# The order of gates, context turns, projection passes and scores in a fused two-block kernel

## The reference, cut to what matters

```python
def first_block(x, mem, ...):
    for i in range(DEPTH):                      # layer A, then layer B
        h = rmsnorm(x, norm_w[i])
        mix, q_mem, gate = gla_mixer(h, ...) if i % 2 == 0 else dilated_mixer(h, ...)
        mem_o = memory_attention(q_mem, mem_n, w_memkv[i])          # softmax(q_mem k) v
        branch = concatenate([mix, mem_o]) * silu(gate)
        x = x + branch @ w_out[i]
    return rmsnorm(x, final_norm_w)

def _layer(x, xc, ...):                          # second block, layer l = 0, 1
    h = _rms(x, g_pre) * (1.0 + scale) + shift                     # latent rows
    hc = _rms(xc, g_pre) * (1.0 + mod_c[1]) + mod_c[0]             # context rows
    ...                                          # h @ w_in, hc @ w_in, split by columns
    # differential attention: two score maps of 48 columns per head
    s1 = einsum('bqhd,bkhd->bhqk', a, k1) * scale
    s2 = einsum('bqhd,bkhd->bhqk', b, k2) * scale
    w = softmax(s1) - lam * softmax(s2)
    o = einsum('bhqk,bkhe->bqhe', w, v)          # then a norm per head, times silu(gate)
    y = concatenate([na, diff, conv]) @ w_out
    x_new = x + gate * _rms(y, g_post)           # and xc in the first layer
```

## Time and profile before

| | |
|---|---|
| median of 3 runs | 1652.66 us (1650.25 to 1654.98) |
| profiled execution | 1653.44 us |
| its span | 1651.6 us |
| mean granted clock of PE | 0.991 |
| PE busy | 1597.0 us (97%), 8870 matmuls |
| DVE busy | 979.8 us (59%) |
| ACT busy | 667.6 us (40%) |
| POOL busy | 140.7 us (9%) |
| mean DMA traffic | 98 GB/s |

### The profile page before, as it was taken

The page is one execution under the profiler, slowest core; times in us unless marked ns, Lnnn a source line. Parts: engine busy times, 40 slices in busy tenths (PEclk is TensorE's granted clock), DMA queues, the critical chain, the costliest instruction groups (busy, mean ns, idle before and its releaser), DMA issues.

```text
span 1651.6 us, 22948 instructions
## 1 busy us (share of the span) xinstructions
PE 1597.0 (97%) x8870; PEld 1277.7 (77%) x8870; DVE 979.8 (59%) x1803; ACT 667.6 (40%) x1323; POOL 140.7 (9%) x192
## 2 busy tenths in 40 slices
PE   7999999899999999999999999989999999999898
PEld 6977877687878878878888888865656887788676
DVE  1356454456556655665447787565665467876674
ACT  3365443424323323263313435244554325433653
POOL 4132100000000000002000110000112001000001
PEclk9999999899999999999999999999999999999899
DMA  8221244334654764462223111221003134213100
GB/s 289 81 77 50 103 153 117 80 82 121 190 158 120 155 185 139 148 151 68 92 96 109 56 54 40 92 93 58 1 26 96 48 107 140 58 39 128 52 14 39
DMA packets 171252, 161.36 MB, mean 98 GB/s; under 512 B 40374, under 2 KB 154280, under 8 KB 171112
## 3 DMA queue, kind: packets, MB, share of 16 engines
q1 hardware_dynamic: 151944, 126.97, 26.1%
q10 hardware_dynamic: 16928, 25.27, 4.7%
q0 software_dynamic: 2272, 7.64, 1.4%
HBM read 149.80 MB, written 11.18 MB: 97 GB/s over the span
## 4 chain that ended last, share of the span: by engine, by line
PE 83%; DVE 10%; ACT 4%; issue 2%; DMA 0%; POOL 0%; ACTq 0%; SPq 0%; POOLq 0%; DVEq 0%
PE psum L2596 46%; PE psum L2567 10%; PE psum L2630 7%; PE psum L3139 5%; PE psum L2621 4%; PE psum L3137 2%; PE psum L2775 2%; PE psum L2687 2%; PE psum L2730 2%; DVE arena L1999 1%; PE psum L2669 1%; PE psum L3010 1%; DVE arena L1969 1%; DVE wring_r L2076 1%; DVE arena L2133 1%
## 5 line engine op out<-in xcount | busy, mean ns | idle before, releaser
L2596 PE MATMUL psum<-hT_r,wring_r 128*128 128x512 f32 x1696 | 575.2, 393 | 3.6 <-ACT branch L1745 1.1
L2596 PEld LDWEIGHTS psum<-hT_r,wring_r 128*128 128x128 f32 x1696 | 319.3, 188 | 79.0 <-issue 10.0
L2596 PE MATMUL psum<-arena_r,wring_r 128*128 128x256 f32 (+1 forms) x1360 | 359.1, 333 | 0.7 <-ACT branch L1564 0.5
L1564 ACT ACTIVATE arena<-psum 128x512 f32<-128x512 f32 (+6 forms) x256 | 149.8, 611 | 416.0 <-PE psum L2596 244.2
L2596 PEld LDWEIGHTS psum<-arena_r,wring_r 128*128 128x128 f32 x1360 | 218.3, 190 | 26.2 <-issue 1.8
L2567 PE MATMUL psum<-arena 128*128 128x96 f32 (+9 forms) x1460 | 220.8, 365 | 16.9 <-ACT branch L1745 7.1
L2596 PE MATMUL psum<-arena_r 128*128 128x512 f32 (+1 forms) x720 | 224.5, 350 | 0.0
L2567 PEld LDWEIGHTS psum<-arena 128*128 128x128 f32 (+5 forms) x1460 | 160.8, 189 | 64.7 <-issue 31.9
L2596 PE MATMUL psum<-hT_r,arena_r 128*128 128x512 f32 x448 | 177.8, 397 | 1.8 <-DVE wring_r L2076 1.0
L2630 PE MATMUL psum<-ident,arena 128*128 128x128 f32 (+3 forms) x1104 | 145.9, 277 | 17.4 <-DMA arena<-in_c_ctx 7.4
L2630 PEld LDWEIGHTS psum<-ident,arena 128*128 128x128 f32 (+3 forms) x1104 | 125.2, 142 | 39.6 <-issue 14.6
(11 more groups left out here) (237 smaller groups left out, 1967.8 us busy)
## 6 DMA issues: line engine op xcount, KB each, us to landing
wring<-in_w_in_b SPq DMA_DIRECT2D x54, 512.0 KB, 5.9
arena<-in_w_mod ACTq DMA_DIRECT2D x16, 1536.0 KB, 8.3
wring<-in_w_in SPq DMA_DIRECT2D x16, 1536.0 KB, 6.9
wring<-in_w_out SPq DMA_DIRECT2D x8, 2048.0 KB, 8.4
wring<-in_w_in_a SPq DMA_DIRECT2D x5, 1536.0 KB, 6.6
arena<-x_dram SPq DMA_DIRECT2D x3, 2048.0 KB, 14.6
wring<-in_w_in SPq DMA_DIRECT2D x6, 1024.0 KB, 5.7
arena<-ebias_dram SPq DMA_DIRECT2D x144, 32.0 KB, 1.8
```

What stands on the lines that cost most here:

```text
L1564: return nc.scalar.activation(out, in_, ACT.Copy, scale=scale)
L2596: ins_ = nc.tensor.matmul(b[0:hi.shape[2], 0:width], w[:, k], v[:, k], start=k + p == 0, stop=(k, p) == (KT - 1, 2))
```

## The change

The diff has eight pieces, none of which changes what is computed:

1. Gate B 4 stands ahead of qm B in the step list, in place of behind it.
2. `final_rows(TT - 2)` on DVE is a step xr of its own ahead of hcT 0; it was part of xf behind it.
3. In layer 1 nv stands ahead of nq.
4. hcT 1 stands behind the last dT of layer 0's differential stage, in place of behind doT of the last row tile. The place from which weight slots are counted for layer 1 stays at that doT.
5. oN stands ahead of yv and the first part of yc, in place of behind them.
6. gate B 0 and the first output of nkc (at even k) run hi x hi and lo x hi as soon as the features' hi is there, and wait for their lo ahead of the third pass.
7. nk does the same for all k, in groups of three outputs.
8. dS claims and fills the banks of one map, then those of the other; before, both were claimed and then the two maps' matmuls alternated.

```diff
--- before.py
+++ after.py
@@ -198,10 +198,9 @@
     add("v" * 8, "wout", "A")
     modulation()
     add("v" * 8, "hT", "B")
-    for i in range(4):
+    for i in range(5):
         add("a", "gate", "B", i)
     add("av", "qm", "B")
-    add("a", "gate", "B", 4)
     add("a" * 8, "mS", "B")
     for g in range(2):
         add("aav", "Bproj", 0, g)
@@ -238,6 +237,7 @@
         add("va", "BPV", h)
     add("", "outs", "wout", "B", 0, (5,))
     add("v" * 6, "wout", "B")
+    add("", "xr")
     add("vvvv", "hcT", 0)
     add("", "xf")
     add("vv", "woutl", "B")
@@ -251,8 +251,11 @@
         for f in range(CF):
             add("av" + "av" * both, "cv", l, f)
         add("av" * 3, "nvF", l)
-        add(lat_ctx * 3, "nq", l)
+        if l == 0:
+            add(lat_ctx * 3, "nq", l)
         add("aaaavv", "nv", l)
+        if l:
+            add(lat_ctx * 3, "nq", l)
         neighbourhood(add, l)
         keys = [("av", "dF", l, "k", g) for g in range(3)]
         queries = [(lat_ctx, "dF", l, "q", g) for g in range(3)]
@@ -495,6 +498,8 @@
             if h == 0 and i:
                 projected(tiles[i - 1])
             add("a", "dT", l, t, h)
+            if n > len(items) and l == 0:
+                add("vvvv", "hcT", 1)
             if n == 4:
                 add("vv", "dv", l, 2)
             rows = [(tiles[i - 1], 1)] if h == 1 and i else [(t, 0)] if n == 5 or (h == DH - 1 and i) else []
@@ -508,6 +513,8 @@
         if n < len(items):
             add("aa", "dS", l, *items[n])
         beside(n)
+        if n >= 2 and h == 0 and i:
+            add("", "oN", l, tiles[i - 1])
         if n >= 2 and l:
             for half, q in YO_SPLITS.get(n, ()):
                 add("", "yv", half, q)
@@ -515,8 +522,6 @@
                 if part == 0:
                     add("", "yc", u, part)
         if n >= 2:
-            if h == 0 and i:
-                add("", "oN", l, tiles[i - 1])
             if h == 1 and i > 1:
                 add("", "yx", l, tiles[i - 2])
             if h == 2 and i > 1 and l == 0:
@@ -537,9 +542,7 @@
     if l == 0:
         add("", "nx", before)
     add("v", "doT", l, last)
-    if l == 0:
-        add("vvvv", "hcT", 1)
-    else:
+    if l:
         add("", "yx", l, before)
     add("v", "yo", l, last, 0, 1)
     add("v", "yo", l, last, 1, 1)
@@ -930,7 +933,7 @@
         split_list = [(key, g) for key, _ in steps for g in range(split_jobs(key))]
         split_at = {job: n for n, job in enumerate(split_list)}
         before_mem = split_at[("Bproj", 1, 0), 0]
-        split_starts = [("wout", "A"), ("wout", "B"), ("hcT", 1)]
+        split_starts = [("wout", "A"), ("wout", "B"), ("doT", 0, TT - 1)]
         split_bounds = [sum(split_jobs(key) for key, _ in steps[:order_of[start]]) for start in split_starts]
 
         def split_place(n):
@@ -2229,8 +2232,9 @@
                         free(nc.vector.scalar_tensor_tensor(branch[:, f], full(dve, key, f)[:, :],
                                                             vec[:, V_GLA + f % 3:V_GLA + f % 3 + 1], branch[:, f],
                                                             ALU.mult, ALU.mult))
+                elif kind == "xr":
+                    final_rows(TT - 2)
                 elif kind == "xf":
-                    final_rows(TT - 2)
                     norm_scale("C0", TT - 2)
                 elif kind in ("wout", "woutl"):
                     ph = key[1]
@@ -2588,11 +2592,17 @@
                 b = claim(pe, key, i) if 0 in blocks else bank(key, i)
                 new = {("gate", "B", 0): ("hT", "B")}.get(key)
                 for k in blocks:
+                    passes = ((hi, x_hi), (hi, x_lo), (lo, x_hi))
                     if key[0] == "nkc" and i == 0 and k % 2 == 0:
-                        evacuated(pe, ("hcT", key[1]), k // 2)
-                    if new and i == 0:
-                        evacuated(pe, new, k)
-                    for p, (w, v) in enumerate(((hi, x_hi), (hi, x_lo), (lo, x_hi))):
+                        turned, last_k, b_ = ("hcT", key[1]), k + 1, k // 2
+                    else:
+                        turned, last_k, b_ = new if i == 0 else None, k, k
+                    if turned:
+                        pe.wait_ge(hi_ready, hi_at(turned, last_k))
+                        passes = ((hi, x_hi), (lo, x_hi), (hi, x_lo))
+                    for p, (w, v) in enumerate(passes):
+                        if turned and p == 2:
+                            evacuated(pe, turned, b_)
                         ins_ = nc.tensor.matmul(b[0:hi.shape[2], 0:width], w[:, k], v[:, k], start=k + p == 0, stop=(k, p) == (KT - 1, 2))
                 if KT - 1 in blocks:
                     done(ins_)
@@ -2681,10 +2691,14 @@
                     parts = [split_weights(split_at[("nkc", l), g])[2:] for g in range(3)]
                     banks = [claim(pe, key, g) for g in range(3)]
                     for k in range(KT):
+                        pe.wait_ge(hi_ready, hi_at(("hT", f"C{l}"), k))
+                        for g, (hi, lo) in enumerate(parts):
+                            nc.tensor.matmul(banks[g], hi[:, k], hT_hi[:, k], start=k == 0, stop=False)
+                        for g, (hi, lo) in enumerate(parts):
+                            nc.tensor.matmul(banks[g], lo[:, k], hT_hi[:, k], start=False, stop=False)
                         evacuated(pe, ("hT", f"C{l}"), k)
                         for g, (hi, lo) in enumerate(parts):
-                            for p, (w, v) in enumerate(((hi, hT_hi), (hi, hT_lo2), (lo, hT_hi))):
-                                ins_ = nc.tensor.matmul(banks[g], w[:, k], v[:, k], start=k + p == 0, stop=(k, p) == (KT - 1, 2))
+                            ins_ = nc.tensor.matmul(banks[g], hi[:, k], hT_lo2[:, k], start=False, stop=k == KT - 1)
                             if k == KT - 1:
                                 done(ins_)
                         if k + HT_BANKS < KT:
@@ -3040,20 +3054,19 @@
                     evacuated(pe, ("dX", l, "q", t))
                     if (t, h) == (0, 0):
                         evacuated(pe, ("dX", l, "k", TT + CT - 1))
-                    for half in range(2):
-                        claim(pe, key, half)
                     tt = t % TT
                     rows = [slice(half * DPAD, half * DPAD + DD) for half in range(2)]
                     q = [dqT[t // TT][r, h, tt * P:(tt + 1) * P] for r in rows]
                     if t < TT:
-                        for part in range(2):
-                            cut = slice(part * KEYS // 2, (part + 1) * KEYS // 2)
-                            for half in range(2):
+                        for half in range(2):
+                            claim(pe, key, half)
+                            for part in range(2):
+                                cut = slice(part * KEYS // 2, (part + 1) * KEYS // 2)
                                 ins_ = product(psum[:, 2 * half + part, 0:KEYS // 2], [(q[half], dkT[rows[half], h, cut])])
-                                if part:
-                                    done(ins_)
+                            done(ins_)
                     else:
                         for half in range(2):
+                            claim(pe, key, half)
                             done(product(psum[:, 2 * half, 0:NMEM], [(q[half], dkT[rows[half], h, T:KEYS])]))
                 elif kind == "dT":
                     l, t, h = key[1:]
```

## The result

The changed kernel takes 1640.69 us (median, 1639.46 to 1641.01), the kernel before 1653.61 in the same comparison. The ratio is 0.992, with an interval of 0.9907 to 0.9934: 12.9 us faster. The forecast was 1640.2.

The account below looks back on a forecast made before the run. PE (TensorE, 83% of the chain) was taken as the bound. The terms -10.3 - 3.25 + 4.9 - 0.4 - 2.8 - 0.6 sum to -12.45 us, from a median of 1652.66 to 1640.2, range 1632 to 1650.

Parts of the forecast that it names:

- gate B 4 ahead of qm: Gate B to Bproj: weights load and are rounded earlier, Bproj starts at about 309.55 instead of 318.09; -10.3 us with the clock.
- rounded half first: gate B 0: Gate B 0: half of PE's 0.93 us wait for VectorE's low half goes; -0.45 us.
- nk, layer 0 and layer 1: First nk matmuls of each layer: six of nine run before the low half comes; -1.4 us per layer.
- final rows ahead of hcT 0: Block 1's final rows: one 1.3 us VectorE operation passes ahead of eight copy pairs; 0, up to 0.5 us cost.
- hcT 1 early: Border before layer 0's last output projection: PE stalls 3.4 us behind VectorE's pairs, lower clock costs 2.0; +4.9 us in all.
- nv ahead of nq: Layer 1 neighbourhood projections: 0.97 us wait for nv's low half replaced by about 0.6 for nvF's copy; -0.4 us.
- oN ahead of yv: Layer 1 differential stage: PE's 2.27 us wait for VectorE's normalisation goes, dT starts 2.4 earlier; -2.8 us.
- map by map: Differential scores: map 0 can run while PE waits for map 1's bank; -0.6 us in all.
- gain of 4 more: Differential scores: possible extra 4 us if the filled waits no longer bring the lower clock.
- (a): Rival: the border costs little and filled waits bring no lower clock; about 1633 us, chance 0.13.
- (b): Rival: Bproj's load is not earlier, as another semaphore than PE's read holds it; 1654.2 us, chance 0.06.
- (c): Rival: score maps lose their overlap, 1.1 us in each of 32 latent items; near 1675 us, chance 0.04.

Follow-up runs that it names:

- fourth experiment: Changed kernel with gate B 4 back behind qm B and the two roundings ahead of its silu moved behind the exponentials of mS: 1640.48 us.
- first two experiments: Changed kernel with hcT 1 back behind doT of the last row tile: 1635.08 us; changed kernel with hcT 1 one output half later: 1641.86 us.
- experiments 3 and 7: Kernel before with only gate B 4 ahead of qm B: 1641.76 us; changed kernel with oN behind yv and yc again: 1644.36 us.
- experiment 1: Changed kernel with hcT 1 back behind doT of the last row tile: 1635.08 us, timed again 1635.31 us.

## Why the prediction was right, point by point

The mechanism was right: PE is the bound, the chain from gate 4's last read to mS gave 10.7 of the 12.4 us of span, and the border took back what was foreseen. That the time was met within 0.5 us is in part luck. Several small terms came out wrong and cancelled (gate B 0, nkc, nv, the maps, 0.8 in layer 0), and the stretches of lower clock in layer 1 differ from trace to trace by more than 0.5 us. This is how each term stands by the aligned traces, with the experiment on it beside it.

| term | forecast | traces | experiment |
|---|---|---|---|
| gate B 4 ahead of qm | -10.3 | -10.7 | -10.65 alone |
| rounded half first: gate B 0 | -0.45 | 0.0 | 0.0 |
| nk, layer 0 and layer 1 | -1.4, -1.4 | -1.6, -1.45 | -5.2 for the piece |
| final rows ahead of hcT 0 | 0 | 0.0 up to matmul 3900 | only with others |
| hcT 1 early | +4.9 | +5.15 | +5.4 to +5.6 |
| nv ahead of nq | -0.4 | -0.1 | -0.7, one run |
| oN ahead of yv | -2.8 | -3.5 with the maps | -2.8 to -3.7 |
| map by map | -0.6 | in the line above | 0.0 |
| not forecast | | +0.6 at the start, -0.8 in layer 0 | |

- **Gate B 4.** The chain was read right: the load waits for PE's last read of gate 4, the rounding for the load, the silu for the rounding, mS for the silu. Once the 0.6 us with which the run started later is taken off, each forecast time is met within about 0.6: rounding at 301.7 (302.90), mS at 305.3 (305.92), Bproj at 309.55 (309.65). The 32 mS matmuls took 3.80 us and not 4.25, which is the 0.4 above the forecast. The fourth experiment adds that either order works if no rounding stands ahead of what PE wants.
- **gate B 0.** The step that failed is "I take half of that": nothing went. The wait of 0.93 had two releasers close together. In the changed kernel it is 0.88 and names a low half of the weights, which the new order of passes doesn't help, since its second pass needs it:

```profile
266.39 0.70 PE L2606 MATMUL psum<-hT_r,wring_r 128*128 128x512 f32 x2 [0.88 <-DVE wring_r L2079]
```

- **nk.** The sentence "The end moves by what runs beneath the wait" gave 1.4, and 1.6 and 1.45 came. Undone, the piece costs more, as its wait can bring the lower clock with it. In the kernel before it had not. To take from one trace that 2.1 us is harmless for the clock was an overreach that did not show in the sum.
- **The border.** Stall 3.47 against 3.4, bare wait 0.81 against 0.75, lower clock 1.6 against 2.0. Of the 0.8 that was to come back at nkc only 0.4 did: from the first of the 12 output matmuls behind doT to matmul 6750 PE took 11.12 us before and 10.73 after. The first two experiments show that it is VectorE's queue.
- **nv.** The two waits went as forecast, and PE is 1.6 us earlier by matmul 7200. By 7500 it has lost 1.45 of that, 1.06 of it in a wait for a norm on VectorE, which the forecast didn't have.
- **oN and the maps.** -3.5 against -3.4, but not split as forecast, and the agreement is luck in part. The maps bring nothing: undone, they move this stage by 0.1 us. So the 3.5 are oN's together with the lower clock, of which the kernel before had 10.2 us in this stage and the changed one 3.4; the traces of experiments 3 and 7 put oN at 1.2 and 2.8. The "gain of 4 more" that was held possible did not come: a stretch of 6.8 us at half clock stands at the context scores in all thirteen traces, in the changed kernel (1097.8 to 1104.6) behind a wait of 0.83 us where it was 1.29.
- **The lower clock.** The prediction has four waits "end in" its four windows of lower clock. Only the first does; those of 1.29, 1.74 and 2.27 us end 0.3 to 0.9 us ahead of theirs. It priced a stretch at half its length. At the border that held, 1.6 us for one of 3.4, but not in layer 1's differential stage, as the last section shows.
- **The rivals.** (a) fell with the stall, (b) with Bproj at 309.65, (c) with 1.57 us for an item. The rule of the Trainium skill by which (c) would have come, page "TensorE: Matmul & The Clock Gate", section on packing small matmuls, does not describe these records: blocks of four took 1.57 us an item and alternating ones 1.56.

With hcT 1 back in its old place, all else changed, the kernel takes 1635.1 and 1635.3 us, and no other that ran was faster beyond its noise.

## What to carry to other kernels

Before work is moved ahead on an engine because it idles there, list what stands behind it in that engine's queue and who waits for that; an idle time of 8 us held 7.4 us of work, and it still stalled PE by 3.5 us, since the work arrived only 2.6 us before the idle time ended. The same holds for a rounding that waits for a DMA: what was queued behind it here, the silu that PE needed, inherited the DMA's wait. A gain worked out for one stage should be followed to the end of the trace: 0.9 us at mS was gone 470 us later, whereas 10.7 us stood.

## What the hardware showed that was not expected

- The lower clock behind a wait differs in length and in whether it comes, for the same wait. Behind the stall of the border it lasted 3.4 us in the changed kernel and about 7 in experiment 4, here with its PEclk and a window that holds it:

```profile
1240.00:1248.00 8.00, 6.82 (x9) 2.93 (x10) 6.36 (x10) 3.99 (x5) 2.06 (x4) 0.57 0.16 66
```

  In the changed kernel the wait of 0.74 us at 1536.75 brought none, and 3.4 us of it came later, from 1545, behind the wait of 1.14 at 1542.50. The kernel of experiment 1 shows both in its own two traces: behind the wait of 0.74 at scores the clock was low for 10.2 us in the first, and not at all in the second:

```profile
1531.50:1541.70 10.20, 10.20 (x34) 7.49 (x34) 9.28 (x19) 8.48 (x21) 1.99 (x2) 0.50 0.43 172
```

```profile
1529.00:1549.00 20.00, 16.58 (x89) 11.80 (x88) 18.92 (x35) 15.55 (x32) 1.98 (x2) 1.00 0.29 106
```

  Yet from matmul 8250 to 8550 the first took only 0.8 us more than the second (57.0 against 56.2), where half of 10.2 would be 5.1. The second had waits of 1.14, 0.57 and 0.97 us there that the first had not. So in this stage the lower clock mostly took the place of waits, and one trace alone does not price it.
- VectorE's low half of 512 columns (line 2135 before), which reads two tensors from arena and hT, takes 0.69 us alone. Beside GpSimd's mask operation of 1.3 us on 128x512 (line 1209) it took longer, 0.88 at 785.84 and 1.51 at 788.93 in the kernel before, 1.77 at most. In the thirteen traces 41 of these instructions start while such an operation runs: 39 of them end 0.55 us behind its end, two 0.63, whenever they started. The other 167 take 0.69 to 0.70. The instruction just before, which reads PSUM and a small tensor, takes 0.80 to 0.81 in either case. These ends fit a low half that gets its data only once GpSimd is through. In experiment 4 the two met at 774.74, and 0.8 us of wait for PE followed.
